# Products of a constant tile in TensorE's waits: at the start of scan and attention, and at the head of each unit of the scan

## What is computed

```python
b = jnp.cumsum(gi, axis=2)
inter = jnp.einsum('bhtk,bhkv->bhtv', qi * jnp.exp(b), state)
decay = jnp.where(lower, jnp.exp(jnp.where(lower, rel, 0.0)), 0.0)
scores = jnp.einsum('bhtk,bhsk,bhtsk->bhts', qi, ki, decay)
intra = jnp.einsum('bhts,bhsv->bhtv', scores, vi)
```

## Time and profile before

| | us |
|---|---|
| median of 3 runs | 3334.11 |
| lowest and highest run | 3331.81, 3337.91 |
| the profiled execution's own time | 3342.67 |
| its span, first to last instruction | 3340.9 |

### The profile page before, as it was taken

The page is one execution under the profiler, slowest core; times in us unless marked ns, Lnnn a source line. Parts: engine busy times, 40 slices in busy tenths (PEclk is TensorE's granted clock), DMA queues, the critical chain, the costliest instruction groups (busy, mean ns, idle before and its releaser), DMA issues. The chain is left out here.

```text
span 3340.9 us, 41079 instructions
## 1 busy us (share of the span) xinstructions
PE 2336.2 (70%) x15570; PEld 1787.1 (53%) x15570; DVE 2034.2 (61%) x4541; ACT 886.0 (27%) x1475; POOL 1438.7 (43%) x1268
## 2 busy tenths in 40 slices
PE   6977899794558787878899998887973433333345
PEld 3777555593357777776778775786553400000001
DVE  3576444399968899878643344665437955655520
ACT  3323134221363333323333333422431100000000
POOL 1034001330007775555655552022036677777764
PEclk8976688896789999988999999886876655556567
DMA  5210141124359999999999996210037799999997
GB/s 202 67 29 1 59 152 47 68 102 151 126 215 407 406 404 362 404 361 398 405 405 406 405 406 266 92 29 8 1 109 267 269 364 339 355 362 362 335 369 265
DMA packets 248756, 816.92 MB, mean 245 GB/s; under 512 B 26776, under 2 KB 45784, under 8 KB 247664
## 3 DMA queue, kind: packets, MB, share of 16 engines
q0 software_dynamic: 147456, 536.94, 42.0%
q1 hardware_dynamic: 101104, 277.35, 22.3%
HBM read 796.37 MB, written 17.83 MB: 244 GB/s over the span
## 5 line engine op out<-in xcount | busy, mean ns | idle before, releaser
L1924 PE MATMUL ps<-sparse_ring,sparse_wdiag 128*32 128x512 f32 x1024 | 226.4, 994 | 405.3 <-DMA sparse_ring<-in_v_rows,eidT 340.7
L2282 POOL DMA_INDIRECT sparse_ring<-in_v_rows,eidT x256 | 287.4, 1123 | 296.3 <-PE ps L2331 217.6
L2091 DVE CUSTOM_DVE_ANT_0 sparse_ring<-sparse_ring,hT 128x1024 f32<-128x1024 f32 x256 | 305.0, 1223 | 166.7 <-DMA sparse_ring<-in_u_rows,eid 160.4
L2282 POOL DMA_INDIRECT sparse_ring<-in_u_rows,eid x256 | 347.0, 1355 | 114.4 <-issue 68.1
L117 PE MATMUL ps<-h_hi,peer_uh 128*128 128x256 f32 x1024 | 310.8, 303 | 90.5 <-DVE peer_ul L2394 81.5
L1924 PEld LDWEIGHTS ps<-sparse_ring,sparse_wdiag 128*32 128x32 f32 x1024 | 44.9, 152 | 575.9 <-issue 575.9
L1886 POOL DMA_INDIRECT sparse_ring<-in_u_rows,eid x256 | 301.3, 1177 | 110.7 <-issue 75.9
L1886 POOL DMA_INDIRECT sparse_ring<-in_v_rows,eidT x256 | 274.7, 1073 | 132.0 <-issue 74.4
L2420 DVE CUSTOM_DVE_ANT_0 sparse_ring<-sparse_ring,hT 128x1024 f32<-128x1024 f32 x256 | 304.0, 1223 | 39.9 <-DMA sparse_ring<-in_u_rows,eid 35.1
L119 PE MATMUL ps<-h_hi,peer_ul 128*128 128x256 f32 x1024 | 299.8, 293 | 2.5 <-issue 2.3
L118 PE MATMUL ps<-h_lo,peer_uh 128*128 128x256 f32 x1024 | 299.8, 293 | 0.0
(11 more groups left out here) (408 smaller groups left out, 5403.6 us busy)
## 6 DMA issues: line engine op xcount, KB each, us to landing
peer_u<-in_uT SPq DMA_DIRECT2D x128, 512.0 KB
peer_v<-in_v_rows SPq DMA_DIRECT2D x128, 512.0 KB
ada_slab<-in_ada_w SPq DMA_DIRECT2D x20, 2048.0 KB, 8.8
proj_slab<-in_w_fm SPq DMA_DIRECT2D x38, 512.0 KB
route_slab<-in_w_pq SPq DMA_DIRECT2D x32, 512.0 KB, 3.3
peer_gates<-dense_stage SPq DMA_DIRECT2D x4, 4096.0 KB, 13.0
peer_gates<-peer_gates SPq DMA_DIRECT2D x32, 512.0 KB
out_slab<-in_w_out SPq DMA_DIRECT2D x16, 512.0 KB, 3.7
```

What stands on the lines that cost most here:

```text
L1924: mm = nc.tensor.matmul(ps[32 * q:32 * (q + 1), 6 + half, :], wdiag[:, q, HQ * half_h + j, :], ring[:, s % R, half * BANK:(half + 1) * BAN ...
L2091: nc.vector.tensor_tensor_reduce(out=ring[:, s % R], in0=ring[:, s % R], in1=hT[:, t], scale=1.0, scalar=0.0, op0=ALU.mult, op1=ALU.add, a ...
L2282: nc.gpsimd.indirect_dma_start(out=ring[:, s % R], out_offset=None, in_=rows, in_offset=bass.IndirectOffsetOnAxis(ap=at, axis=0)).then_inc ...
```

## The change

`ones` becomes a tile of type FP32r (a one-pass form of FP32 on TensorE), set by VectorE from `meanD`; all old readers read the same tile as FP32. A new helper issues a product of that tile with itself, 128 rows, 128 weight columns and 512 moving columns (the tile repeated four times), into a PSUM bank from which nobody reads it. It is called at three places: 24 times at the start of TensorE's stream in the scan, 24 times in attention between the sums and the wait for `n_done`, and once at the head of each of the 8 units of each pair, behind `bank_free` and ahead of the wait for `ready`. That is 24 + 24 + 32 = 80 products in a layer and 160 in all. The product of a unit goes into the unit's own first bank, which the unit then overwrites.

```diff
@@ constants
-        ones = sb(ctx, "ones", [P, P])
+        ones_r = sb(ctx, "ones", [P, P], F32R)
+        ones = f32(ones_r[:])
@@ phase_start, VectorE
-                        nc.vector.memset(ones[:], 1.0)
-                        nc.vector.memset(meanD[:], 1.0 / D_MODEL).then_inc(mean_set, 1)
+                        dve_chain(dve, nc.vector.memset(meanD[:], 1.0 / D_MODEL))
+                        nc.vector.tensor_scalar(ones_r[:], meanD[:], float(D_MODEL), None, ALU.mult).then_inc(mean_set, 1)
@@ new helper
+        def keep_busy(bank, times):
+
+            for _ in range(times):
+                nc.tensor.matmul(ps[:, bank, :], ones_r[:], bc(ones_r[:], 1, BANK // P), start=True, stop=True)
@@ phase_scan, TensorE, scores(pr)
                                 bank_free(n)
                                 bank_free(n + 1)
+                                keep_busy(n % RB, 1)
                                 if pr == first[c] and u in (0, 3):
...
+                        keep_busy(7, 24)
                         for pr in range(4):
                             scores(pr)
@@ phase_attn, TensorE
-                        nc.tensor.matmul(ps[:, 1, :], ones[:], sq[:, 2], start=True, stop=True).then_inc(sum_done, 1)
+                        nc.tensor.matmul(ps[:, 1, :], ones, sq[:, 2], start=True, stop=True).then_inc(sum_done, 1)
+                        keep_busy(7, 24)
                         pe.wait_ge(n_done, 1)
```

More of the change, by code:

```diff
@@ L663, in gates @@
                                 for t in range(TT):
-                                    nc.vector.tensor_tensor_scan(cum[:, s, t, 1:P + 1], ones[:], log_decay[s][:, t * P:(t + 1) * P],
+                                    nc.vector.tensor_tensor_scan(cum[:, s, t, 1:P + 1], ones, log_decay[s][:, t * P:(t + 1) * P],
                                                                  0.0, ALU.mult, ALU.add)
@@ L1146, in _ @@
                         pe.wait_ge(sq_done, 1)
-                        nc.tensor.matmul(ps[:, 0, lo:], ones[:], sq[:, 0, lo:], start=True, stop=False)
+                        nc.tensor.matmul(ps[:, 0, lo:], ones, sq[:, 0, lo:], start=True, stop=False)
                         nc.tensor.matmul(ps[:, 0, lo:], ones[0:64, :], sq[0:64, 1, lo:], start=False, stop=True)
-                        nc.tensor.matmul(ps[:, 1, :], ones[:], sq[:, 2], start=True, stop=True).then_inc(sum_done, 1)
+                        nc.tensor.matmul(ps[:, 1, :], ones, sq[:, 2], start=True, stop=True).then_inc(sum_done, 1)
+                        keep_busy(7, 24)
                         pe.wait_ge(n_done, 1)
```

## The result

| | before | changed |
|---|---|---|
| median, us | 3334.36 (4 runs) | 3387.20 (4 runs) |
| lowest and highest run | 3331.81, 3337.91 | 3376.24, 3391.90 |
| the profiled execution, its span | 3342.67, 3340.9 | 3376.24, 3374.4 |

The ratio is 1.0156, with an interval of 1.0134 to 1.0178: 53 us or 1.6% slower, where 1.3% was forecast. The profiled execution of the changed kernel is the fastest of its four.

What follows compares the result with a forecast made beforehand. TensorE at its low 1.2 GHz clock was taken to bound the scan; 38.4 us for products in units plus 1.8 and 2.6 made 42.8, added to the 3334.1 us median: 3377 us, 1.3% slower, range 3346 to 3390.

Steps and rivals of the forecast that it cites:

- The clock stays low in the units: Scan units of both layers: TensorE stays at 1.2 GHz despite a product at each head; forecast chance 0.80.
- The starts buy nothing: Starts of scan and attention: products fit in waits, some 8, 4 and 4 to 5 us stay idle, nothing gained or lost.
- Rival B: Start of attention alone runs at 2.4 GHz: 16 us less, 3361 us, or 3341 with products at 0.43 us; chance 0.05.
- How many lie on the path: Products at unit heads that lengthen the scan: 25 in layer 0, 23 in layer 1, together 48.
- The price: One product at a unit's head: 0.8 us taken, between bounds of 0.43 and 0.93; 38.4 us for 48.
- the two small terms: Scan: 1.8 us where units 1 and 2 exceed TensorE's slack, 2.6 us for lost overlap between pairs 0 and 1.
- The term for the lost overlap: Between pairs 0 and 1: twelve records no longer run beside the last joining matmuls, 1.3 us in each layer.
- The execution it was made against: Durations came from an execution of 3342.67 us, 8.6 us above the median, taken to lie outside the stretches at issue.
- rival C: The products vanish in waits that the records hide: within 0.2%, 3336 us; chance 0.05.
- rival A: The products raise the clock in the scan and hold it: 64 us faster, 3270 us; chance 0.08, half-way cases 0.02.

Runs made afterwards that it cites:

- e3: Changed kernel with two products instead of one at the head of each unit; 3362.33 us, ratio 1.0228 to the kernel before.
- e7: Kernel before plus products in the scan's long waits, three (layer 1: two) ahead of units in pairs 0 and 1, one in pairs 2 and 3; ratio 1.0031.
- e6: Kernel before plus products only at the start of the scan, 64 in layer 0 and 40 in layer 1; 3288.97 us, ratio 1.0004.
- e12: e9 with no product ahead of layer 1's units and 50 instead of 40 at layer 1's attention; 3313.89 us, ratio 0.9950 to the kernel before.
- e1: Changed kernel without the products at the heads of units, only those at the starts of scan and attention; 3288.52 us, ratio 1.0007 to the kernel before.
- e5: Kernel before plus 44 products at the start of attention, none elsewhere; 3278.08 us, ratio 0.9967.
- e4: Changed kernel with each unit's product only on the rows of the pair's first head (32 or 64); 3306.40 us, ratio 1.0057 to the kernel before.
- e2: Changed kernel with only the products at the heads of units, none at the starts; 3342.01 us, ratio 1.0161 to the kernel before.
- e8: e7 plus 44 products at the start of attention; 3283.28 us, ratio 0.9977 to the kernel before.
- e9: Kernel before plus products in waits of pairs 2 and 3, one ahead of each of their units, 44 (layer 1: 40) at attention's start; 3308.19 us, ratio 0.9916.
- e10: e9 without the product ahead of each unit; 3317.11 us, ratio 0.9949 to the kernel before.

## Why the prediction was right, and which terms were off

**The clock stays low in the units: right.** 0.50 in the window of pairs 0 and 1, and e3 and e7 show that two and three products to 32 records do not change it there. That TensorE without a gap does not by itself have the clock is shown once more by e6 and by layer 0 of e7, where it was lost without one. This is the step on which the sign rested. The strip of rows 1 was read a little too low (slices 3 to 5 show 7, 6 and 6 tenths); nothing hangs on it, since the windows give the 0.50.

The Trainium skill (TensorE: Matmul & The Clock Gate, HAM oscillation — how this bites in real kernels) explains a clock that swings by waits for data between bursts of matmuls. The runs agree for the longer waits (3.67 us in e12, 6.34 and 6.29 in the changed kernel); e6 and e7 show the clock lost without any wait, which differs, and the measurement decides.

**The starts buy nothing: right.** 8.47 and 3.14 us were left in the scans (8 and 4 forecast), 6.29 and 3.52 in attention (4 to 5 forecast), and e1 puts all of them at +0.5 us by the medians and +2 by the ratio, with an interval of -2 to +7. Rival B was not far away, though: e5, with 20 products more in the same place, is what it describes, at -12 us (-16 forecast for 24 products that hold the clock).

**How many lie on the path: right.** 48 places; e3's second products, at 0.43 us, give 20.3 us for the 48 x 0.43 = 20.6. The first product of pair 2 stands ahead of no wait of its own (the earlier trace rows show none), but the wait for the first copy, three units later, takes it up.

**The price: mis-sized.** The step was "A pair of L973 records (0.21 us) spends up to half its time on its own load, which is then counted twice, so 0.93 - 0.1 = 0.8 us is the value I take". It measured 0.92 in both layers: 0.43 for the columns and 0.49 for leaving and entering the units' rows (e3, e4). The upper bound, two changes of rows at the 0.25 us of L1157 and L1158, was the value, and there was nothing to take off. 48 x 0.92 = 44.2, with the two small terms of 1.8 and 2.6 us 48.6 (49.4 with the slack worked out at 0.92 as well, 2.6 for 1.8); the stretches show 48.5. As the sum for each layer, 23.0 + 1.0 + 1.3 = 25.3 for 24.5 measured and 21.2 + 0.8 + 1.3 = 23.3 for 24.0. The term for the lost overlap can be seen in the timeline, in which the products of L1002 and the next pair's L980 no longer stand side by side as those of the earlier trace rows (251.54) did. From the first unit to the first output product of layer 0 it is 75.65 us for 60.21, 15.4 more; 15 products at 0.92 are 13.8 of it, which leaves 1.6 for a term taken at 1.3. No run tested it alone.

**The execution it was made against.** The remark that the 8.6 us above the median lay outside the stretches holds: outside them the two profiled executions differ by 15 us, more than twice what the price was off (48 x 0.12 = 5.8 us), and the stretches are where a change is to be read.

**Against rival C,** the products hidden: e2's 54 us. **Against rival A:** in layer 0 nothing brought the 32-row units to keep 2.4 GHz, not even three products to a unit. In layer 1 of e7 and e8 two products to 16 records, begun at a high clock, did keep it, so its mechanism exists; but a unit with its products then took 1.70 us for 1.71, so holding the clock paid for itself and no more. Whether the change's one product to 16 records would keep a clock that is high when pair 0 begins was not tried, since the products of the start ended too early.

## What to carry to other kernels

A filler product is free only where the engine waits, and useful only where it lasts nearly to the end of the wait; 24 of them brought nothing and 44 in the same place 12 us. How many that takes depends on the clock they run at, so look at more than one execution. At the head of a unit that bounds the time it costs its columns and the change of rows, which here was the larger half. If one is put there, it wants the rows of its neighbours (0.43 in place of 0.92 us), and it belongs only in units whose clock it keeps at less than the clock gives back. The 64-row units of layer 0 behind filled waits were such a place: with the start of attention they made 22 to 28 us of gain (e9) out of 53 us of loss, and 14 to 17 where the start of attention fell back (e12). The 32-row units of layer 1 were not: two products kept their clock and cost what it gave.

## What the runs showed of the hardware

- A product over 128 rows between matmuls over 32 or 64 costs 0.92 us at 1.2 GHz; on the neighbours' rows 0.43; a second one behind it 0.43.
- The granted clock falls under matmuls that follow each other without a gap: under 32-row units alone (e6, 0.72 in the window of 224 to 228 us) and with three full-width products to 32 records (0.93, then 0.50, layer 0 of e7). Two products to 16 records of 32 rows kept it for 31 us (1.00, layer 1 of e7). One product for 32 records of 64 rows kept it for 74 us (e7), one for 16 records in layer 1 did not always (in e9 the units from 2283 us on are at 1.97 us for 16 records, those up to 2280 us at 1.11).
- What was left of attention's wait behind the products, and the queries behind it: with 0.32 to 0.97 us (layer 0 of e5, e8, e9, e10) all of them ran at 2.4 GHz; with 1.86 to 3.21 (layer 1 of e12, e9, e10) the first one to four rows did and then no more; with 3.52 to 6.29 (the changed kernel, e12's layer 0, e1) none did.
- The same instructions give the high clock in one execution and the low one in another (L1169 at 1.10 in e9, 2.02 in e12), so one profile of such a place says little about its median; how often each comes was not measured.
